# A block inverse by doubling: narrow column updates, a turned transpose, and scores issued first in each level

## The chip, the cores and the metric

The kernel runs on one core of a Trainium2 chip. The metric is device time of the whole program in microseconds (us); one launch computes everything.

## The reference, cut to what matters

The reference is two stacked networks over 256 tokens of width 1024. The change touches one mixer of the first, `even_mixer`, which runs once. Of it two parts matter: an attention of 8 heads of 64, and a gated delta rule of 4 heads of 128, whose core is a unit lower triangular solve.

```python
decay = jnp.exp(jnp.where(tri, gc[..., :, None] - gc[..., None, :], -jnp.inf))
a_mat = jnp.where(strict, jnp.einsum('bnhid,bnhjd->bnhij', k_beta, kc) * decay, 0.0)
t_mat = a_mat + jnp.eye(B_CHUNK, dtype=a_mat.dtype)
u = lax.linalg.triangular_solve(t_mat, vc * bc, left_side=True, lower=True, unit_diagonal=True)
w = lax.linalg.triangular_solve(t_mat, k_beta * jnp.exp(gc)[..., None], left_side=True, lower=True,
                                unit_diagonal=True)
```

The kernel takes chunks of 128 tokens instead of 64, which is the same function: two chunks T0 and T1, four heads each, so eight 128x128 matrices (I + A), and it needs the inverse X of each.

## The kernel before

Everything is float32. Each engine runs its own list of instructions in the order in which the code writes it, and semaphores join the lists; nothing is scheduled by a planner. In the mixer the functions are all called `even()`, one for each engine: ScalarE (L1034), VectorE (L1848), TensorE (L2729).

The inverse is built by doubling. For level 0 X = I - A masked to the pairs of rows. At level l (1 to 6) blocks of 2^l rows that are already inverted are joined in pairs: with `off` = A masked to the lower left quarters of the pairs (VectorE, `off(T, level)`, L1893), X becomes X - X (off X). The kernel keeps X in `d_X` and its transpose in `d_XT`, since a product on TensorE takes its left operand transposed as the weights. A level is, for each T:

- TensorE: Y = off X, four heads of 128 columns, into one PSUM bank (`LEV_Y`), L2875.
- ScalarE: copy of Y to SBUF (`quarter_copy`, L1087 to 1090), 128x512.
- TensorE: the product that changes XT (bank `LEV_XT`) and, up to level 5, the one that changes X (`LEV_X`), four heads each.
- VectorE: XT minus its bank (L1972), X minus its bank (L1974).

`each(bank, fn)` calls fn for the four heads, `product` (L2751) is one fp32 matmul of 128x128 by 128 columns and `turned` (L2754) one transpose against the identity. The trace shows an fp32 matmul as two passes, each a weight load and a matmul record, and a transpose as one.

Into these levels the attention heads are woven, one per level: `scores(i)` (TensorE, L2773 and 2774, weights of 64 rows), `masked(i)` (VectorE, L1867 to 1870: scale, mask and row maxima), `exps(i)` (ScalarE, L1078), `turn_p(i)` (TensorE, L2780, three transposes), `p_copy(i)` (ScalarE, L1085), `weigh(i)` (TensorE, L2788 to 2790, 64 columns), `head_out(i)` (VectorE, L1875 to 1877). TensorE's order in a level is Y of T0, Y of T1, `weigh(level)`, `scores(level + 1)`, XT and X of T0, the same of T1, `turn_p(level + 1)`.

The weights of the large projections come through a ring of seven 1 MB slots (`RING`), filled by the SP queue in order; a slot is loaded anew once ScalarE and VectorE have split both its halves, called granules, into a high part (`hi(k)`, L844) and a low part (`lo(k)`, L1595). On VectorE one `lo(2)` stands ahead of `masked(1)`, before the levels; it splits granules 2 and 3 of the mixer's output projection, which TensorE uses after the levels. Before the first level VectorE also copies X (L1963) from the PSUM banks 0 and 1, where TensorE has turned it from XT.

After the levels the products U and W are formed from XT (L2751 again, with `d_vb` and `d_kbg`), then the state, the normalisation and the output projection; then the feed-forward layer.

Of the kernel before, what the change touches and what calls it, by code (L numbers as in the profile page):

```python
# [24 lines left out]
ALU = mybir.AluOpType  # L25
ACT = mybir.ActivationFunctionType
# [143 lines left out]
def build_block_kernel(nc, t, const, out):  # L170

    ctx = ExitStack()
    with ctx:
# [271 lines left out]
        d_vn = [quarter(RAW, 0), buf(xt, 3)]  # L445
        d_S, d_U, d_W = quarter(RAW, 1), quarter(RAW, 5), buf(xt, 2)
        LEV_Y, LEV_XT, LEV_X = (4, 3), (2, 5), (0, 1)

        o_z = scr[:, 0:4096].rearrange("p (b n) -> p b n", b=TB)
        o_x = scr[:, 4096:8192].rearrange("p (b n) -> p b n", b=TB)  # L450
# [379 lines left out]
        def _(act):  # L830
# [203 lines left out]
            def even():  # L1034
# [39 lines left out]
                def exps(i):  # L1074

                    act.wait_ge(at_mx, n(at_mx))
                    for tb, k in ((0, slice(0, P)), (1, slice(P, 3 * P))):
                        ins = act.activation(a_s[:, i % 2, k], a_s[:, i % 2, k], ACT.Exp,  # L1078
                                             bias=w8(30 + i % 2, 2)[:, tb:tb + 1], accum_out=w8(32 + i % 2, 2)[:, tb:tb + 1])
                    ins.then_inc(at_p, 1)  # L1080

                def p_copy(i):

                    act.wait_ge(at_pt, n(at_pt))
                    act.activation(a_pt[:, i % 2, :], ps[:, 7, 0:384], ACT.Copy).then_inc(at_pc, 1)  # L1085

                def quarter_copy(dst, bank, wait, done):  # L1087

                    act.wait_ge(wait, n(wait))
                    act.activation(dst, ps[:, bank, :].rearrange("p (c n) -> p c n", c=4), ACT.Copy).then_inc(done, 1)  # L1090
# [74 lines left out]
                exps(0)  # L1165
                hi(2)
                p_copy(0)
                exps(1)
                p_copy(1)
                for level in range(1, 7):  # L1170
                    for T in range(TB):
                        quarter_copy(d_Y[T], LEV_Y[T], dl_y, dl_yc)
                    exps(level + 1)
                    p_copy(level + 1)
                n(dl_u)
# [382 lines left out]
        def _(dve):  # L1558
# [30 lines left out]
            def lo(k):  # L1589

                for g in range(gp[0] + ahead[0], gp[0] + k):
                    s = g // 2
                    c, width, o = granule(s, g % 2)
                    dve.wait_ge(hi_done, n.gran(g + 1))
                    dve.tensor_tensor(w_lo[:, g % SPLITS, 0:c * width], w_raw[:, s % RING, o:o + c * width],  # L1595
                                      w_hi[:, g % SPLITS, 0:c * width].bitcast(F32), ALU.subtract).then_inc(lo_done, 1)
                    if layer[0] is not None and at_sum[0] < (48 if layer[0] else 64):
                        credit[0] += SUM_RATE[layer[0]]
                        if credit[0] >= 1:
                            credit[0] -= 1  # L1600
                            accumulate(layer[0], at_sum[0])
                            at_sum[0] += 1
                gp[0] += k
                ahead[0] = 0
# [243 lines left out]
            def even():  # L1848
# [14 lines left out]
                def masked(i):  # L1863

                    dve.wait_ge(at_sc, n(at_sc))
                    m = w8(30 + i % 2, 2)
                    link(dve.scalar_tensor_tensor(a_s[:, i % 2, :], ps[:, 6, 0:384], A_DIM ** -0.5, e_mask, ALU.mult, ALU.add))  # L1867
                    dve.tensor_reduce(m[:, 0:1], a_s[:, i % 2, 0:P], AX_X, ALU.max)
                    link(dve.tensor_reduce(m[:, 1:2], a_s[:, i % 2, P:384], AX_X, ALU.max))
                    dve.tensor_scalar(m, m, -1.0, None, ALU.mult).then_inc(at_mx, 1)  # L1870

                def head_out(i):

                    dve.wait_ge(at_pv, n(at_pv))
                    link(dve.reciprocal(w8(34 + i % 2, 2), w8(32 + i % 2, 2)))  # L1875
                    for tb in range(TB):
                        ins = dve.tensor_scalar(xn[:, tb, i * A_DIM:(i + 1) * A_DIM], ps[:, 7, 384 + tb * A_DIM:384 + (tb + 1) * A_DIM],
                                                w8(34 + i % 2, 2)[:, tb:tb + 1], None, ALU.mult)
                    ins.then_inc(at_o, 1)
# [4 lines left out]
                def heads(b):  # L1884
                    return ps[:, b, :].rearrange("p (c n) -> p c n", c=4)
# [7 lines left out]
                def off(T, level):  # L1893

                    dve.tensor_tensor(d_off[T][level % 2], d_A[T], bc_mid(lev[:, level, :], 4), ALU.mult).then_inc(dl_off, 1)
# [60 lines left out]
                    dve.tensor_tensor(d_XT[T], bc_mid(ident, 4), d_Y[T], ALU.subtract).then_inc(dl_xt, 1)  # L1956
                    off(T, 1)
                head_out(0)
                lo(2)
                masked(1)  # L1960
                for T in range(TB):
                    dve.wait_ge(dl_xtt, n(dl_xtt))
                    dve.tensor_copy(d_X[T], heads((0, 1)[T])).then_inc(dl_x, 1)  # L1963
                for level in range(1, 7):
                    if level < 6:
                        off(0, level + 1)
                        off(1, level + 1)
                    head_out(level)
                    masked(level + 1)
                    for T in range(TB):  # L1970
                        dve.wait_ge(dl_xy, n(dl_xy))
                        ins = dve.tensor_tensor(d_XT[T], d_XT[T], heads(LEV_XT[T]), ALU.subtract)  # L1972
                        if level < 6:
                            ins = dve.tensor_tensor(d_X[T], d_X[T], heads(LEV_X[T]), ALU.subtract)  # L1974
                        ins.then_inc(dl_x, 1)
                dve.wait_ge(dl_u, 1)
                dve.tensor_copy(d_vn[0], heads(4)).then_inc(dl_vn, 1)
                head_out(7)
# [532 lines left out]
        def _(pe):  # L2511
# [217 lines left out]
            def even():  # L2729
# [14 lines left out]
                def each(bank, fn):  # L2744

                    for i in range(B_HEADS):
                        ins = fn(i, ps[:, bank, i * P:(i + 1) * P])
                    return ins

                def product(a, b):  # L2750
                    return lambda i, o: pe.matmul(o, a[:, i, :], b[:, i, :], start=True, stop=True)  # L2751
# [116 lines left out]
                pe.wait_ge(at_o, 1)  # L2868
                turn_p(1)

                for level in range(1, 7):
                    for T in range(TB):
                        pe.wait_ge(dl_off, n(dl_off))
                        pe.wait_ge(dl_x, n(dl_x))
                        each(LEV_Y[T], product(d_off[T][level % 2], d_X[T])).then_inc(dl_y, 1)  # L2875
                    weigh(level)
                    pe.wait_ge(at_mx, level + 1)
                    scores(level + 1)
                    for T in range(TB):
                        pe.wait_ge(dl_yc, n(dl_yc))  # L2880
                        ins = each(LEV_XT[T], product(d_Y[T], d_XT[T]))
                        if level < 6:
                            ins = each(LEV_X[T], product(d_XT[T], d_Y[T]))
                        ins.then_inc(dl_xy, 1)
                    pe.wait_ge(at_o, level + 1)
                    turn_p(level + 1)
# [557 lines left out]
```

## Time and profile before

| | |
|---|---|
| runs | 2714.8, 2716.03, 2716.27 us; median 2716.03 |
| profiled execution | 2714.96 us, span in the profile 2712.8 us |
| TensorE busy | 2622.0 us, 97% of the span, 12546 matmul records |
| VectorE, ScalarE busy | 2042.1 us (75%), 1681.3 us (62%) |
| DMA | 687.42 MB, mean 253 GB/s |
| the levels of the inverse | 328.15 to 375.71 us of the span |

The span begins with the first instruction and ends with the last one; the device time has 2.2 us around it. "PE" is TensorE's matmul, "PEld" its weight load, DVE is VectorE, ACT ScalarE. A number in brackets at the end of a timeline row is idle time of that engine before the row, with the instruction that ended it. The granted clock is the share of 2.4 GHz that TensorE got: 1.00, or 0.50 for 1.2 GHz. Matmuls overlap, so their lengths do not add up; the starts of the weight loads give TensorE's pace.

### The profile page before, as it was taken

To read this page: it belongs to the slowest core of one execution; us is meant where nothing else is said; L and a number is where in the kernel's file an instruction comes from. 1 tells how busy PE (TensorE), PEld (TensorE's weight loads), DVE (VectorE), ACT (ScalarE), POOL (GpSimd) and SP (SyncE) were. 2 spreads that over 40 slices of the span, in tenths; PEclk is the share of its full clock that TensorE was granted. 3 is DMA by queue.
4 is the path that set the end of the run, shared out by engine and by line. 5 is a ranking of instruction groups with operands and counts; after the bars stand their busy time and mean duration, and the time that the engine had idled before them with its cause. 6 is when DMAs were issued, how large, how long until landed. Compare 5 with 4: busy or idle time off the path is not lost.

```text
span 2712.8 us, 35093 instructions
## 1 busy us (share of the span) xinstructions
PE 2622.0 (97%) x12546; PEld 2159.3 (80%) x12546; DVE 2042.1 (75%) x2376; ACT 1681.3 (62%) x2188; POOL 155.0 (6%) x196
## 2 busy tenths in 40 slices
PE   7999899999999999999989999999999999999997
PEld 6888787888887887888767888788887878888886
DVE  4556657777766765554577875799999999999998
ACT  4446645454456765454464444678788787878786
POOL 2000000000000000003310000300000000000020
PEclk9999999999999999999999999899999999999999
DMA  8554306768744346754128884699999999999995
GB/s 291 190 171 163 109 32 241 248 223 299 261 162 158 125 130 238 269 172 138 63 84 307 314 289 148 225 378 372 367 387 362 388 357 378 372 378 373 361 390 223
DMA packets 284412, 687.42 MB, mean 253 GB/s; under 512 B 13428, under 2 KB 21904, under 8 KB 284304
## 3 DMA queue, kind: packets, MB, share of 16 engines
q1 hardware_dynamic: 266032, 618.65, 63.7%
q0 software_dynamic: 18272, 67.32, 7.0%
q8 instruction: 69, 1.13, 0.2%
q14 instruction: 39, 0.32, 0.0%
HBM read 670.19 MB, written 15.73 MB: 253 GB/s over the span
## 4 chain that ended last, share of the span: by engine, by line
PE 84%; DVE 8%; ACT 5%; issue 2%; DMA 0%; DVEq 0%; SPq 0%; ACTq 0%; POOL 0%
PE ps L2519 26%; PE ps L2521 25%; PE ps L2520 25%; DVE w_lo L1595 2%; PE ps L2667 2%; ACT w_hi L844 2%; PE ps L2751 1%; DVE xt L2365 1%; DVE xn L1674 1%; DVE h L1679 1%; PE ps L3137 0%; DVE act_lo L1663 0%; ACT hp L1257 0%; PE ps L3203 0%; PE ps L2726 0%
## 5 line engine op out<-in xcount | busy, mean ns | idle before, releaser
L1595 DVE TENSOR_TENSOR w_lo<-w_raw,w_hi 128x1024 fp32r<-128x1024 f32 x1158 | 1397.4, 1226 | 424.3 <-ACT w_hi L844 394.1
L844 ACT ACTIVATE w_hi<-w_raw 128x1024 fp32r<-128x1024 f32 x1158 | 1211.7, 1057 | 773.4 <-PE ps L2521 772.8
L2519 PE MATMUL ps<-w_hi,act_hi 128*128 128x512 f32 (+1 forms) x3424 | 1343.9, 392 | 39.0 <-DVE w_lo L1595 23.3
L2521 PE MATMUL ps<-w_lo,act_hi 128*128 128x512 f32 (+1 forms) x3424 | 1321.8, 386 | 0.0
L2520 PE MATMUL ps<-w_hi,act_lo 128*128 128x512 f32 (+1 forms) x3424 | 1320.4, 386 | 0.0
L2519 PEld LDWEIGHTS ps<-w_hi,act_hi 128*128 128x128 f32 x3424 | 646.8, 189 | 183.6 <-DVE w_lo L1595 36.8
L2521 PEld LDWEIGHTS ps<-w_lo,act_hi 128*128 128x128 f32 x3424 | 646.4, 189 | 131.5
L2520 PEld LDWEIGHTS ps<-w_hi,act_lo 128*128 128x128 f32 x3424 | 647.2, 189 | 123.4 <-issue 1.4
L1586 DVE SCALAR_TENSOR_TENSOR scr<-scr,small 128x1024 f32<-128x1024 f32 x98 | 125.2, 1278 | 0.0
L1002 ACT ACTIVATE act_hi<-ps 128x512 fp32r<-128x512 f32 (+1 forms) x87 | 62.5, 719 | 64.2 <-PE ps L2667 64.2
L1720 DVE TENSOR_TENSOR act_lo<-ps,act_hi 128x512 fp32r<-128x512 f32 (+1 forms) x87 | 74.0, 850 | 34.7 <-ACT act_hi L1002 34.7
L647 POOL DMA_DIRECT2D scr<-in_ada_w x48 | 33.9, 706 | 844.7 <-DVE scr L1586 458.6
L2667 PEld LDWEIGHTS ps<-cst,hp 128*128 128x128 f32 x456 | 54.0, 140 | 21.1 <-DVE hp L1743 6.9
L2667 PE MATMUL ps<-cst,hp 128*128 128x128 f32 x456 | 64.5, 273 | 6.0 <-DVE hp L1743 5.4
L1743 DVE SCALAR_TENSOR_TENSOR hp<-ps,rn,sg 128x512 f32<-128x512 f32 (+1 forms) x48 | 31.7, 701 | 36.7 <-PE ps L2521 36.7
L1747 DVE TENSOR_TENSOR hp<-sg,ps 128x512 f32<-128x512 f32 (+1 forms) x63 | 46.6, 739 | 8.1 <-PE ps L2521 8.1
L780 POOL TENSOR_TENSOR dtw<-dtw 128x4 f32<-128x4 f32 x1 | 0.8, 827 | 853.7 <-DMA rows_out<-scr 853.7
L1024 ACT ACTIVATE sg<-ps 128x512 f32<-128x512 f32 (+1 forms) x63 | 39.6, 629 | 0.1
L1020 ACT ACTIVATE sg<-ps,rn 128x512 f32<-128x512 f32 (+1 forms) x48 | 28.3, 639 | 11.4 <-PE ps L2521 11.4
L887 ACT ACTIVATE act_hi<-ps,colv 128x128 fp32r<-128x128 f32 x96 | 26.5, 375 | 9.4 <-PE ps L2549 9.4
L1663 DVE SCALAR_TENSOR_TENSOR act_lo<-ps,colv,act_hi 128x128 fp32r<-128x128 f32 x96 | 26.3, 341 | 3.2 <-ACT act_hi L887 3.2
L2230 DVE TENSOR_REDUCE small<-ps 128x2 f32<-128x1024 f32 x16 | 19.4, 1220 | 7.2 <-PE ps L3203 6.9
(513 smaller groups left out, 1419.5 us busy)
## 6 DMA issues: line engine op xcount, KB each, us to landing
w_raw<-in_moe_w SPq DMA_DIRECT2D x337, 1024.0 KB, 6.8
scr<-in_ada_w POOLq DMA_DIRECT2D x48, 1024.0 KB, 6.7
w_raw<-in_ffn_w_gate SPq DMA_DIRECT2D x44, 1024.0 KB, 5.3
w_raw<-in_ffn_w_up SPq DMA_DIRECT2D x44, 1024.0 KB, 5.6
w_raw<-in_ffn_w_down SPq DMA_DIRECT2D x44, 1024.0 KB, 5.0
w_raw<-in_ff_w SPq DMA_DIRECT2D x42, 1024.0 KB, 5.5
w_raw<-in_odd_w_in SPq DMA_DIRECT2D x20, 1024.0 KB, 5.2
w_raw<-in_even_w_in SPq DMA_DIRECT2D x14, 1024.0 KB, 5.2
```

The lines of the kernel that those rows point to most:

```text
L647: pool.dma_start(m_w[:, j % 2], src).then_inc(ada_in[j % 2], 16)
L844: act.activation(w_hi[:, g % SPLITS, 0:c * width], w_raw[:, s % RING, o:o + c * width], ACT.Copy).then_inc(hi_done, 1)
L1002: act.activation(act_hi[:, base:base + c, 0:tbs * P], src, ACT.Copy).then_inc(hhi_done, 1)
L1024: act.activation(sg[:, 0:tbs * BANK].rearrange("p (b n) -> p b n", b=tbs)[:, :, 0:width], ps[:, 4:4 + tbs, 0:width], ACT.Silu).then_inc(si ...
L1586: dve.scalar_tensor_tensor(dst, w, x, dst, ALU.mult, ALU.add).then_inc(ada_sum, 1)
L1595: dve.tensor_tensor(w_lo[:, g % SPLITS, 0:c * width], w_raw[:, s % RING, o:o + c * width], w_hi[:, g % SPLITS, 0:c * width].bitcast(F32), ...
L1720: dve.tensor_tensor(act_lo[:, base:base + c, 0:tbs * P], src, act_hi[:, base:base + c, 0:tbs * P].bitcast(F32), ALU.subtract).then_inc(hlo ...
L1747: dve.tensor_tensor(view[0], view[1], ps[:, 6:6 + tbs, 0:width], ALU.mult).then_inc(hid_done, 1)
L2519: pe.matmul(out_ap, hi, whi, start=start, stop=False)
L2520: pe.matmul(out_ap, lo, whi, start=False, stop=False)
L2521: return pe.matmul(out_ap, hi, wlo, start=False, stop=stop)
L2667: ins = pe.transpose(banks(6, tbs)[:, o:o + P], hp[:, tb * BANK + k * P:tb * BANK + k * P + P], ident)
```

## The change

X is updated only in the columns that a level changes. Of each pair of blocks these are the columns of the first block, `first_columns(x, level)`: runs of 2^level columns out of every 2^(level+1), 64 of a head's 128 at every level. Y = off X is formed for them alone, into half a bank, packed; ScalarE copies the 64 columns per head (`d_Yc`); the X product is formed from them, and VectorE subtracts 128x256 numbers in place of 128x512. The XT product goes. Instead TensorE turns X (`turned(d_X[T])`) from level 2 on, right behind Y of the same T, and ScalarE copies the turned matrix to `d_XT`. At level 6 only the lower left 64x64 of X is missing, and it is subtracted straight from XT, rows 0 to 63 and columns 64 to 127.

The first copies of X go from VectorE to ScalarE. TensorE issues `scores(level + 1)` first in a level, and VectorE runs `masked(level + 1)` ahead of `off` and `head_out(level)`. The `lo(2)` ahead of `masked(1)` goes to level 6, in the place of `off`.

```diff
--- before.py
+++ after.py
@@ -445,6 +445,20 @@
         d_vn = [quarter(RAW, 0), buf(xt, 3)]
         d_S, d_U, d_W = quarter(RAW, 1), quarter(RAW, 5), buf(xt, 2)
         LEV_Y, LEV_XT, LEV_X = (4, 3), (2, 5), (0, 1)
+        LEVELS = 6
+        d_Yc = [y[:, :, 0:64] for y in d_Y]
+
+        def first_columns(x, level):
+
+            return x.rearrange("p c (b two s) -> p c b two s", two=2, s=1 << level)[:, :, :, 0, :]
+
+        def packed(x, level):
+
+            return x.rearrange("p c (b s) -> p c b s", s=1 << level)
+
+        def half_bank(b):
+
+            return ps[:, b, 0:256].rearrange("p (c n) -> p c n", c=4)
         o_z = scr[:, 0:4096].rearrange("p (b n) -> p b n", b=TB)
         o_x = scr[:, 4096:8192].rearrange("p (b n) -> p b n", b=TB)
@@ -1165,11 +1179,16 @@
                 exps(0)
                 hi(2)
                 p_copy(0)
+                for T in range(TB):
+                    quarter_copy(d_X[T], T, dl_xtt, dl_x)
                 exps(1)
                 p_copy(1)
-                for level in range(1, 7):
+                for level in range(1, LEVELS + 1):
                     for T in range(TB):
-                        quarter_copy(d_Y[T], LEV_Y[T], dl_y, dl_yc)
+                        act.wait_ge(dl_y, n(dl_y))
+                        act.activation(d_Yc[T], half_bank(LEV_Y[T]), ACT.Copy).then_inc(dl_yc, 1)
+                        if level > 1:
+                            quarter_copy(d_XT[T], LEV_XT[T], dl_xtt, dl_yc)
                     exps(level + 1)
                     p_copy(level + 1)
                 n(dl_u)
@@ -1956,23 +1975,22 @@
                     dve.tensor_tensor(d_XT[T], bc_mid(ident, 4), d_Y[T], ALU.subtract).then_inc(dl_xt, 1)
                     off(T, 1)
                 head_out(0)
-                lo(2)
                 masked(1)
-                for T in range(TB):
-                    dve.wait_ge(dl_xtt, n(dl_xtt))
-                    dve.tensor_copy(d_X[T], heads((0, 1)[T])).then_inc(dl_x, 1)
-                for level in range(1, 7):
-                    if level < 6:
+                for level in range(1, LEVELS + 1):
+                    masked(level + 1)
+                    if level < LEVELS:
                         off(0, level + 1)
                         off(1, level + 1)
+                    else:
+                        lo(2)
                     head_out(level)
-                    masked(level + 1)
                     for T in range(TB):
                         dve.wait_ge(dl_xy, n(dl_xy))
-                        ins = dve.tensor_tensor(d_XT[T], d_XT[T], heads(LEV_XT[T]), ALU.subtract)
-                        if level < 6:
-                            ins = dve.tensor_tensor(d_X[T], d_X[T], heads(LEV_X[T]), ALU.subtract)
-                        ins.then_inc(dl_x, 1)
+                        if level < LEVELS:
+                            x, y = first_columns(d_X[T], level), packed(half_bank(LEV_X[T]), level)
+                        else:
+                            x, y = d_XT[T][0:64, :, 64:128], half_bank(LEV_X[T])[0:64]
+                        dve.tensor_tensor(x, x, y, ALU.subtract).then_inc(dl_x, 1)
                 dve.wait_ge(dl_u, 1)
                 dve.tensor_copy(d_vn[0], heads(4)).then_inc(dl_vn, 1)
                 head_out(7)
@@ -2868,19 +2886,32 @@
                 pe.wait_ge(at_o, 1)
                 turn_p(1)
-                for level in range(1, 7):
-                    for T in range(TB):
-                        pe.wait_ge(dl_off, n(dl_off))
-                        pe.wait_ge(dl_x, n(dl_x))
-                        each(LEV_Y[T], product(d_off[T][level % 2], d_X[T])).then_inc(dl_y, 1)
-                    weigh(level)
+                def narrow(bank, level, fn):
+
+                    for i in range(B_HEADS):
+                        ins = fn(i, packed(half_bank(bank), level)[:, i])
+                    return ins
+
+                for level in range(1, LEVELS + 1):
                     pe.wait_ge(at_mx, level + 1)
                     scores(level + 1)
                     for T in range(TB):
-                        pe.wait_ge(dl_yc, n(dl_yc))
-                        ins = each(LEV_XT[T], product(d_Y[T], d_XT[T]))
-                        if level < 6:
-                            ins = each(LEV_X[T], product(d_XT[T], d_Y[T]))
+                        off, x, xt_, y = d_off[T][level % 2], first_columns(d_X[T], level), d_XT[T], d_Yc[T]
+                        pe.wait_ge(dl_off, n(dl_off))
+                        pe.wait_ge(dl_x, n(dl_x))
+                        narrow(LEV_Y[T], level, lambda i, o: pe.matmul(o, off[:, i, :], x[:, i], start=True, stop=True)).then_inc(dl_y, 1)
+                        if level > 1:
+                            each(LEV_XT[T], turned(d_X[T])).then_inc(dl_xtt, 1)
+                    weigh(level)
+                    for T in range(TB):
+                        off, x, xt_, y = d_off[T][level % 2], first_columns(d_X[T], level), d_XT[T], d_Yc[T]
+                        pe.wait_ge(dl_yc, n(dl_yc, 2 if level > 1 else 1))
+                        if level < LEVELS:
+                            ins = narrow(LEV_X[T], level,
+                                         lambda i, o: pe.matmul(o, xt_[:, i, :], packed(y, level)[:, i], start=True, stop=True))
+                        else:
+                            ins = narrow(LEV_X[T], level,
+                                         lambda i, o: pe.matmul(o[0:64, 0], y[:, i, :], xt_[:, i, 64:128], start=True, stop=True))
                         ins.then_inc(dl_xy, 1)
                     pe.wait_ge(at_o, level + 1)
                     turn_p(level + 1)
```

## Rows read from the trace of the kernel before

**Rows 1.** The page, the chain that ended last: shares of the span by engine.
```profile
PE 84%; DVE 8%; ACT 5%; issue 2%; DMA 0%; DVEq 0%; SPq 0%; ACTq 0%; POOL 0%
```

**Rows 2.** Busy time by stretch: columns as printed; then granted clock, DMA share, GB/s.
```profile
core 0: us, PE busy (x) PEld busy (x) DVE busy (x) ACT busy (x) POOL busy (x), PEclk, DMA share, GB/s
309.40:311.90 2.50, 2.50 (x23) 2.50 (x24) 0.18 (x1) 2.50 (x7) 0.00 (x0) 1.00 0.01 3
321.60:331.80 10.20, 4.74 (x21) 4.37 (x22) 7.70 (x15) 2.07 (x6) 0.00 (x0) 0.50 0.33 104
345.01:352.85 7.84, 7.59 (x64) 7.03 (x63) 5.76 (x13) 2.67 (x7) 0.00 (x0) 1.00 0.01 3
250.30:253.30 3.00, 3.00 (x29) 3.00 (x29) 2.81 (x4) 3.00 (x7) 0.00 (x0) 1.00 0.01 3
```

**Rows 3.** Timeline of one level, weight loads: start, length, line, count, idle before.
```profile
352.85 0.36 PEld L2780 LDWEIGHTS ps<-cst,scr 128*128 128x128 f32 x3
353.18 0.97 PEld L2751 LDWEIGHTS ps<-scr 128*128 128x128 f32 x8
...
354.56 0.97 PEld L2751 LDWEIGHTS ps<-xt 128*128 128x128 f32 x8 [0.41 <-issue]
355.45 0.30 PEld L2788 LDWEIGHTS ps<-scr 128*128 128x128 f32 x2
355.67 0.30 PEld L2789 LDWEIGHTS ps<-scr 128*128 128x128 f32 x2
...
356.26 0.29 PEld L2773 LDWEIGHTS ps<-scr 64*128 64x128 f32 x2
...
357.11 1.86 PEld L2751 LDWEIGHTS ps<-scr 128*128 128x128 f32 x16 [0.33 <-issue]
```

**Rows 4.** Timeline of the front, to the load of `turn_p(2)`.
```profile
323.35 2.35 DVE L1595 TENSOR_TENSOR w_lo<-w_raw,w_hi 128x1024 fp32r<-128x1024 f32 x2
...
325.61 0.55 DVE L1867 SCALAR_TENSOR_TENSOR scr<-ps,scr 128x384 f32<-128x384 f32 x1
...
327.05 0.40 ACT L1078 ACTIVATE scr<-scr,small 128x128 f32<-128x128 f32 x1 [7.72 <-DVE small L1870]
...
328.15 0.50 PEld L2780 LDWEIGHTS ps<-cst,scr 128*128 128x128 f32 x3 [5.14 <-issue]
...
328.63 1.83 PEld L2751 LDWEIGHTS ps<-scr 128*128 128x128 f32 x8
...
337.18 0.36 PEld L2780 LDWEIGHTS ps<-cst,scr 128*128 128x128 f32 x3
```

**Rows 5.** Whole run, groups by shape: busy us, mean ns, idle before.
```profile
L1221 ACT ACTIVATE xt<-ps,colv 128x256 f32<-128x256 f32 x16 | 7.7, 562 | 3.2 <-PE ps L2937 3.2
...
L1244 ACT ACTIVATE xt<-ps 128x256 f32<-128x256 f32 x4 | 1.5, 364 | 0.0
...
L2081 DVE SCALAR_TENSOR_TENSOR act_lo<-ps,colv,act_hi 128x256 fp32r<-128x256 f32 x12 | 5.0, 476 | 0.0
```

**Rows 6.** Timeline of the level of rows 3, ScalarE and VectorE.
```profile
354.38 0.60 ACT L1090 ACTIVATE scr<-ps 128x512 f32<-128x512 f32 x1 [0.40 <-PE ps L2751]
...
357.22 0.56 DVE L1867 SCALAR_TENSOR_TENSOR scr<-ps,scr 128x384 f32<-128x384 f32 x1 [0.17 <-PE ps L2774]
...
358.46 0.17 DVE L1870 TENSOR_SCALAR small<-small 128x2 f32<-128x2 f32 x1
```

**Rows 7.** Timeline of weight loads, an 8-column projection, at half clock.
```profile
253.66 0.33 PEld L2519 LDWEIGHTS ps<-w_hi,act_hi 128*128 128x128 f32 x1
253.88 0.33 PEld L2520 LDWEIGHTS ps<-w_hi,act_lo 128*128 128x128 f32 x1
```

**Rows 8.** Timeline of weight loads, `turn_p(6)` and the first product after the loop.
```profile
368.51 0.36 PEld L2780 LDWEIGHTS ps<-cst,scr 128*128 128x128 f32 x3
...
375.71 0.97 PEld L2751 LDWEIGHTS ps<-sg,scr 128*128 128x128 f32 x8
```

**Rows 9.** The page, DMA issues: count, size of one, median us to landing.
```profile
w_raw<-in_ffn_w_gate SPq DMA_DIRECT2D x44, 1024.0 KB, 5.3
```

## The prediction

> **What bounds the kernel now.** I read the page first, then the timeline of the stretch in which the changed lines run (about 323 to 376 us), then its clock, then what each engine waits for there. The page's chain [rows 1] gives TensorE 84% of the time, so the kernel is one long stream of TensorE work; the inverse is only some 50 us of 2713, and what the change is worth is decided there alone. One level of the loop repeats every 7.84 us at full clock with TensorE busy 7.59 of it [rows 2]. The reader can lay the level out by the starts of the weight loads [rows 3]: three transposes `turn_p` at 352.85; Y of T0 at 353.18 (eight loads in 0.97, so 0.111 a pass, 0.89 for four fp32 products of two passes each); a stall of 0.49 until VectorE has written X of T1; Y of T1 at 354.56, 0.89; `weigh` at 355.45, products of 64 columns; `scores` at 356.26; the XT and X products from 357.11, 32 passes in 3.57. Sum: 0.33 + 0.89 + 0.49 + 0.89 + 0.81 + 0.85 + 3.57 = 7.83. So a level is bound by TensorE's passes, with one short wait.
>
> The first level is another matter [rows 4]. VectorE splits two weight granules (`lo(2)`, 323.35, 2.35 us) ahead of `masked(1)` (325.61). ScalarE's exponentials wait for that (327.05), and TensorE's `turn_p(1)` waits for them (328.15, after 5.14 us without a load). In this idle time the granted clock is at half, 1.2 GHz, and stays there to 331.8 (0.50 over 321.6 to 331.8 [rows 2]), 3.65 us after TensorE resumed.
>
> **Part 1: what a narrow product costs.** The change makes Y and X 64 columns wide. The price of a pass is what matters, and the nearest row is `weigh`, which also moves 64 columns through 128x128 weights: L2788 begins at 355.45, L2789 at 355.67, so 0.22 for two passes, the same 0.111 as 128 columns [rows 3]. With 8 columns TensorE still makes 29 loads in 3.00 us, about 0.107 apart (250.3 to 253.3 [rows 2]). So halving the columns saves nothing by itself: a narrow product stays at 0.22. Bounds: not below that; above it, if reading every other run of X (`first_columns`, runs of 2 to 64 elements) is slow, up to a doubled 0.44. No row has such a stepped operand; I take 0.22, the row it is nearest to.
>
> **Part 2: what goes and comes on TensorE per level (2 to 5).** Removed: eight wide XT products, 8 x 0.22 = 1.78. Added: eight transposes, 8 x 0.11 = 0.89 (three of them take 0.33 at 352.85 [rows 3]). So the passes fall by 0.89. `scores` moves to the front of the level and the turns lie between the two Y, which together cover what was the stall for X of T1 (0.49 gone). The 64-row weights of `scores` load only as the last matmul before them ends: 0.15 later than the spacing alone behind `weigh` (355.45 + 3 x 0.22 = 356.11 against 356.26 [rows 3]); behind the three transposes I count 0.19. New level: `turn_p` 0.33, drain 0.19, `scores` 0.85, Y 0.89, transposes 0.44, Y 0.89, transposes 0.44, `weigh` 0.67, X 0.89 + 0.89 = **6.48 us**, 1.35 less than 7.83.
>
> Is anything else late in 6.48? Count from `turn_p`'s first load. ScalarE: Y of T0 is finished near 2.5 and copied as 128x256 (0.36 to 0.56 by forms of that size [rows 5]; a 512-element copy takes 0.60 [rows 6], so I take 0.39) to about 2.95; XT of T0 to 3.6; Y and XT of T1 to 4.3 and 4.9. X of T0 starts at 4.70 and of T1 at 5.59, so both are covered, T1 by 0.7. Behind these four copies stand the exponentials, 1.1 us with their read-outs to the load they release (327.05 to 328.15 [rows 4]): to 6.0, and the next `turn_p` is due at 6.48, 0.5 of room. VectorE: `masked` from 1.5, 1.4 long (357.22 to 358.46 and 0.17 [rows 6]), two masks `off` 1.3, `head_out` after `weigh` to about 5.7, then the two X updates of 128x256 at 0.42 (0.48 by the nearest form [rows 5]) to 6.2 and 7.2; the next Y of T0 wants the first at 7.85. So it stays with TensorE. If the ScalarE copies take 0.56 instead of 0.39 the room falls to 0.1 and costs nothing. Four levels: 4 x 1.35 = **5.4 us**.
>
> **Part 3: the front.** `lo(2)` leaves its place, so `masked(1)` starts 2.26 us earlier (325.61 - 323.35 [rows 4]), and with it the exponentials and `turn_p(1)`: load at 325.89 for 328.15. The X copies that go from VectorE to ScalarE (two of 0.60) run at 319.8 and 323.5, where ScalarE is idle before the exponentials. **2.26 us** gained.
>
> **Part 4: level 1 and the clock.** Before, from `turn_p(1)` to `turn_p(2)` it took 9.03 (328.15 to 337.18 [rows 4]), nearly four microseconds of it at half clock: the sixteen Y passes took about 0.21 each (the first eight loads in 1.83). Narrow passes double at half clock too: of the 8-column passes two loads lie 0.22 apart at 253.66 and 253.88 [rows 7], half as far until 253.3 [rows 2]. When does the clock rise now? If at the same instant as before (331.8): `turn_p` 0.48 and its drain 0.35, `scores` 1.5, both Y 3.45, then at full clock `weigh` 0.7 and X 1.78: 8.3 us, `turn_p(2)` at 334.2. If as long after the resumption as before (3.65 us, at 329.5): about 1.0 less. There is no XT turn in level 1. I take the late end, **0.75 us** gained, as the low stretch began before the part that changes; the early end would give 1.75.
>
> **Part 5: level 6 and `lo(2)`'s new place.** Before: 7.2 us from `turn_p(6)` at 368.51 to the first product after the loop at 375.71 [rows 8]. Now `turn_p`, drain, `scores`, Y, turns and `weigh` reach 4.70; the X products with 64 columns of weights have no row: between 0.45 and 0.89 for each T. VectorE: `masked(7)` to 2.95, `lo(2)` 2.35 to 5.3, `head_out(6)` 0.7 to 6.0, the update of T0 to 6.4. So here VectorE ends last, and the product after the loop starts at 6.45 whichever X costs. **0.75 us** gained. The moved `lo(2)` frees a slot of the weight ring some 38 us later, and SP's load behind it starts that much later; it is a slot of the second gate step of the feed-forward, needed after 400, and one such load lands in 5.3 us [rows 9], so it is hidden. TensorE wants these two granules only after the loop.
>
> **The sum.** 2.26 + 0.75 + 5.4 + 0.75 = 9.2 us. The profiled execution took 2714.96, which gives 2705.8; the median of the runs shown is 2716.03, 1.1 higher, which gives 2706.8. I forecast **2706.3**. What follows the loop (the state chain, then the feed-forward, TensorE-bound) shifts as a whole.
>
> **Rival 1, slower: the clock falls inside the loop.** Each new level consists of 64-column passes and transposes. At 253.3 the clock fell with TensorE never idle, after a run of nothing but 8-column passes [rows 2, 7]: a busy engine with thin work can lose it. If it fell for the whole loop, a level would cost double its passes: about 12.2 us, 4.4 more than 7.83. Four such levels, +17.5, level 6 +4, less 3.0 at the front: +18.5, **2734**. It decides from about two levels: each low level turns 1.35 gained into 4.4 lost. Against it: 24 transposes and nothing else between 309.4 and 311.9 ran at a granted 1.00 [rows 2], and the new level has no idle time, with wide `scores` in it. 7%.
> The Trainium skill ("TensorE: Matmul & The Clock Gate", Part 4: PE-mode transpose) says that transposes do not count as work for the clock gate as matmuls do. By that rule the eight new transposes would thin the level further and the time would be this rival's 2734; the stretch from 309.4 does not bear it out.
>
> **Rival 2, no change: stepped reads are slow.** If every Y pass on every other run takes twice its slot, Y costs 1.78 more per level: 5 x 1.78 = 8.9 less gain in levels 2 to 6 and some 1 in level 1: **2716**, same as before. For it: no row shows such an operand. Against: a 64-column pass needs half the time that its slot has (128 columns fit in it), so a doubled read would still fit. If it bites only where runs are 2 or 4 long, 2 to 3 us go. 7% in full.
>
> **Rival 3: the loop becomes a chain of hand-overs.** The four copies, exponentials and `turn_p` have 0.5 of room. If copies and hand-overs together cost 1.2 more than I count, the level is 7.2 and the gain 2.26 + 4 x 0.63 + 1.0 = 5.8: **2710**. For it: five hand-overs in a row in each level. Against: the copies are shorter than before. 14%.
>
> **Chances.** Forecast 72%, rival 1 7%, rival 2 7%, rival 3 14%. This kernel's runs tell a change from none at about 0.2%, 5.4 us. The forecast and three quarters of rival 3 lie beyond it: 0.82 faster; rival 2 and the rest of rival 3, 0.11 same; rival 1, 0.07 slower. Range: if the shorter idle time left the clock at full for all of level 1 (5.7 in place of 8.3, 2.6 more gained), the time were 2703.2 from the profiled execution, and the low end is a little below; rival 3 reaches to 2711.5, part of rival 2 with it.
>
> **What the changed profile would show.** The first load of `turn_p` repeats every 6.5 us in levels 2 to 5 (right) or 7.2 and more (rival 3, with ScalarE's exponentials as the releaser). Eight loads of a narrow Y in 0.97 (part 1), or 1.9 at a clock of 1.00 (rival 2). The first load of `turn_p(1)` near 325.9. A granted clock of 1.00 from 331.8 on to the end of the loop; 0.50 there is rival 1. No idle time before Y of T1. In level 6, VectorE's update as the releaser of the first product behind the loop, near 366.5. The prediction is wrong if a narrow pass is not 0.111, if the clock falls between 332 and 367, or if TensorE stands later for the moved weight load.

## The result, and the profile after

The changed kernel takes 2726.26 us in the median of 20 runs (2718.36 to 2737.47), the kernel before 2714.37 (2711.38 to 2719.47): a ratio of 1.0047, 95% interval 1.0033 to 1.0060, so 12 us slower. The forecast was 2706.3. The 20 runs fall in two groups, eleven of 2718.4 to 2726.3 and nine of 2733.4 to 2737.5; the profiled execution, 2734.03 us, is of the slower group, and e5 below has one of the faster.

The page of the changed kernel, its span, busy times, the granted clock in 40 slices and the chain's shares:

```profile
span 2732.2 us, 35013 instructions
...
PE 2646.1 (97%) x12506; PEld 2179.4 (80%) x12506; DVE 2032.8 (74%) x2364; ACT 1685.7 (62%) x2200; POOL 152.7 (6%) x196
...
PEclk9999869999999999999999999999999999999999
...
PE 85%; DVE 8%; ACT 5%; issue 2%; DMA 0%; DVEq 0%; SPq 0%; ACTq 0%; POOL 0%
```

Fewer matmul records than before (12506 for 12546) and yet 24 us more of busy TensorE. The sixth digit of the clock row is a 6; that slice is 342 to 410 us, and the loop lies in and ahead of it.

Busy time by stretch in the changed kernel (columns as in [rows 2]); level 1 with the 1.2 us ahead of it, level 2, level 6, and the whole low stretch:

```profile
324.10:335.70 11.60, 10.33 (x45) 9.38 (x45) 3.71 (x11) 3.11 (x11) 0.00 (x0) 0.50 0.01 1
335.70:347.71 12.01, 12.01 (x55) 11.03 (x56) 4.02 (x11) 3.33 (x9) 0.00 (x0) 0.50 0.00 0
...
383.73:394.57 10.84, 10.84 (x55) 9.62 (x56) 5.07 (x11) 3.32 (x9) 0.00 (x0) 0.50 0.30 96
324.10:395.80 71.70, 70.43 (x316) 64.33 (x317) 25.26 (x67) 20.03 (x57) 0.00 (x0) 0.50 0.05 15
```

TensorE is never idle in levels 2 to 6, but at a clock of 0.50. Levels 2 to 5 take 12.0 us each, where the kernel before needed 7.84 [rows 2]. The low clock lasts from 324.1 to 395.8, 71.7 us; before it lasted 10.2. It ends 0.75 us after the first product behind the loop (395.05).

Level 3 of the changed kernel, weight loads, to be read beside [rows 3]:

```profile
347.71 0.66 PEld L2798 LDWEIGHTS ps<-cst,scr 128*128 128x128 f32 x3
348.69 0.50 PEld L2791 LDWEIGHTS ps<-scr 64*128 64x128 f32 x2 [0.33 <-issue]
...
350.27 1.78 PEld L2902 LDWEIGHTS ps<-scr 128*128 128x128 f32 x8 [0.65 <-issue]
351.82 0.87 PEld L2772 LDWEIGHTS ps<-cst,scr 128*128 128x128 f32 x4
352.67 1.83 PEld L2902 LDWEIGHTS ps<-xt,scr 128*128 128x128 f32 x8
354.27 0.87 PEld L2772 LDWEIGHTS ps<-cst,xt 128*128 128x128 f32 x4
...
356.41 1.83 PEld L2911 LDWEIGHTS ps<-scr 128*128 128x128 f32 x8
358.12 1.83 PEld L2911 LDWEIGHTS ps<-scr,xt 128*128 128x128 f32 x8
359.71 0.44 PEld L2798 LDWEIGHTS ps<-cst,scr 128*128 128x128 f32 x2
```

Eight loads of a narrow product span 1.83 us, 0.21 apart, twice the 0.97 of [rows 3]: the same passes, each half as fast. The order is the new one (`turn_p`, `scores`, Y, turn, Y, turn, `weigh`, X, X).

The front, to be read beside [rows 4] (ScalarE's second copy of X, VectorE's start of `masked(1)`, the exponentials, the loads of `turn_p(1)` and of `turn_p(2)`):

```profile
322.45 0.60 ACT L1104 ACTIVATE xt<-ps 128x512 f32<-128x512 f32 x1 [2.66 <-PE ps L2772]
322.81 0.55 DVE L1886 SCALAR_TENSOR_TENSOR scr<-ps,scr 128x384 f32<-128x384 f32 x1
...
324.24 0.40 ACT L1092 ACTIVATE scr<-scr,small 128x128 f32<-128x128 f32 x1 [1.19 <-DVE small L1889]
...
325.34 0.50 PEld L2798 LDWEIGHTS ps<-cst,scr 128*128 128x128 f32 x3 [3.16 <-issue]
...
335.70 0.66 PEld L2798 LDWEIGHTS ps<-cst,scr 128*128 128x128 f32 x3
```

The longest sum of waits within the loop (engine, line, for whom; total, times, longest), ScalarE's copy of Y:

```profile
ACT scr L1189 <- PE ps L2902: 24.2, 12, 3.0
```

It waits for TensorE, as VectorE does, while TensorE has from 328 on only short gaps between weight loads, 0.7 us at most, and none of them ends on another engine: no hand-over is late.

### The profile page after: what moved, and what is told of

Its sections match the earlier page's. It is cut to its first block, busy times and chain, and to the rows that moved or that the text cites. A ratio compares the mean times of both kernels' runs of the same rounds, so it can differ in the third digit from the quotient of the medians.

```text
span 2732.2 us, 35013 instructions
## 1 busy us (share of the span) xinstructions
PE 2646.1 (97%) x12506; PEld 2179.4 (80%) x12506; DVE 2032.8 (74%) x2364; ACT 1685.7 (62%) x2200; POOL 152.7 (6%) x196
## 4 chain that ended last, share of the span: by engine, by line
PE 85%; DVE 8%; ACT 5%; issue 2%; DMA 0%; DVEq 0%; SPq 0%; ACTq 0%; POOL 0%
PE ps L2537 26%; PE ps L2539 25%; PE ps L2538 25%; DVE w_lo L1614 2%; PE ps L2685 2%; ACT w_hi L858 2%; PE ps L2902 1%; DVE xt L2383 1%; PE ps L2911 1%; DVE xn L1693 1%; DVE h L1698 1%; PE ps L3168 0%; DVE act_lo L1682 0%; ACT hp L1276 0%; PE ps L3234 0%
## 5 line engine op out<-in xcount | busy, mean ns | idle before, releaser
L1034 ACT ACTIVATE sg<-ps,rn 128x512 f32<-128x512 f32 (+1 forms) x48 | 28.3, 639 | 11.3 <-PE ps L2539 11.3
```

## Experiments

All times are medians; each ratio is to runs of the kernel before on the same chip. Each experiment has one profiled execution, so a stretch shown is that execution's; where the runs of a kernel lie close together, it can stand for them. Two theories stood at first. **A**: the clock is lost in the idle time ahead of level 1, as it was before, and passes of 64 columns do not bring it back; where it is at full, they keep it. **B**: the passes of 64 columns lose it by themselves. **C**, the rival to both: the clock is not the point, but the order, the turned transpose or the moved split.

**e1: the same passes, 128 columns wide.**

```diff
-narrow(LEV_Y[T], level, lambda i, o: pe.matmul(o, off[:, i, :], x[:, i], start=True, stop=True)).then_inc(dl_y, 1)
+each(LEV_Y[T], product(off, d_X[T])).then_inc(dl_y, 1)
...
 if level < LEVELS:
-    ins = narrow(LEV_X[T], level,
-                 lambda i, o: pe.matmul(o, xt_[:, i, :], packed(y, level)[:, i], start=True, stop=True))
+    ins = each(LEV_X[T], product(xt_, d_Y[T]))
 else:
-    ins = narrow(LEV_X[T], level,
-                 lambda i, o: pe.matmul(o[0:64, 0], y[:, i, :], xt_[:, i, 64:128], start=True, stop=True))
+    ins = each(LEV_X[T], product(d_Y[T], xt_))
```

These are TensorE's lines. ScalarE's copy of Y is 128x512 again, and VectorE subtracts the same 64 columns, read out of a full bank.

> The changed kernel with its Y and X products over all 128 columns of a head again (same number of products and passes); the numbers outside the changed columns are computed and not used. The copy of Y is 128x512 again, VectorE subtracts the 64 columns only. Theory A (the clock is lost in the idle time ahead of level 1 and passes of 64 columns cannot raise it again) and theory B (passes of 64 columns lose it by themselves): the clock is back at 1.00 some 7 us after the loop begins, at full clock a level takes 6.5 us, the kernel 2705 to 2707. Theory C (the lost time is the order of the loop, the turned transpose or the moved split, not the width): still slower than the kernel before, 2720 or more.

Measured: 2706.0 us against 2713.76, ratio 0.9974 (0.9962 to 0.9985). Busy time by stretch, the low stretch at the front, then two levels:

```profile
319.80:326.60 6.80, 4.65 (x17) 3.70 (x18) 3.01 (x10) 1.63 (x6) 0.00 (x0) 0.50 0.01 2
329.67:336.15 6.48, 6.48 (x55) 5.98 (x54) 4.02 (x11) 3.53 (x9) 0.00 (x0) 1.00 0.00 0
336.15:342.64 6.49, 6.49 (x55) 5.99 (x54) 4.02 (x11) 3.52 (x9) 0.00 (x0) 1.00 0.00 0
```

The clock is down for 6.8 us, 319.8 to 326.6, and a level takes 6.48. Theory C is out: order, turns and moved split are all in this kernel, and it is 20 us faster than the changed one. What differs is the width, in the direction of more arithmetic (with it ScalarE's copy, for which TensorE does not wait in the levels of either kernel). All seven runs lie at 2704.6 to 2707.8, all 20 of the changed kernel at 2718.4 or more.

**e2: wide fillers ahead of level 1, the narrow loop kept.**

```diff
+for _ in range(8):
+    pe.matmul(ps[:, 5, :], ones, d_A[0].rearrange("p c n -> p (c n)"), start=True, stop=True)
 for level in range(1, LEVELS + 1):
```

> The changed kernel with eight useless fp32 matmuls of 512 columns ahead of level 1, in a free PSUM bank; they cost 6.8 us at half clock, 3.4 at full. Theory A: they raise the clock, the narrow levels then hold it at 1.00, 6.5 us each, and the kernel takes about 2709, faster than before although it does more. Theory B: the clock is raised and falls again within one or two levels, levels of 12 us, 2735 or more.

Measured: 2713.4 us against 2713.76, ratio 0.9998 (0.9989 to 1.0007). Busy time by stretch, the low stretch, level 2, level 6:

```profile
321.10:331.30 10.20, 6.86 (x13) 3.44 (x14) 3.16 (x10) 2.07 (x6) 0.00 (x0) 0.50 0.01 2
340.78:347.13 6.35, 6.35 (x56) 5.85 (x56) 4.02 (x11) 3.32 (x9) 0.00 (x0) 1.00 0.00 0
...
366.18:372.02 5.84, 5.84 (x56) 5.20 (x56) 4.66 (x11) 3.32 (x9) 0.00 (x0) 1.00 0.01 3
```

The fillers cost more than I had counted: 9.5 us (326.23 to 335.75, level 1 with them 15.3) for a counted 6.8 at most. Eight fp32 matmuls are 16 passes, and a pass of 512 columns takes 0.43 us at full clock (e6's loads at 315.85 and 316.28); the expectations here and of e6 took 0.43 for a whole matmul. So the time is 4 us over the expected 2709. What decides between A and B is the clock: it rises under the fillers, at 331.3, and stays at 1.00 through the narrow levels, 6.35 us each, and 5.84 up to `turn_p(7)` in the last. B is out.

**e3: transposes as fillers, and e9: narrow products as fillers**, in the same place, 32 passes each.

```diff
+for _ in range(8):
+    each(5, turned(d_A[0]))
```

```diff
+for _ in range(4):
+    each(5, lambda i, o: pe.matmul(o[:, 0:64], d_A[0][:, i, :], d_A[0][:, i, 0:64], start=True, stop=True))
```

> The same with 32 useless transposes of 128x128 in place of the eight matmuls, as long at half clock (32 x 0.213 = 6.8 us). If transposes count for the clock as products do: the same picture as with the matmuls, the clock at 1.00 before or early in level 1 (about 2709 under theory A). If they do not: the clock stays at 0.50 through the loop, and the kernel takes the changed kernel's time and 6.8 us more, 2730 to 2744.

> The same place as the useless matmuls and the useless transposes, with 16 useless fp32 products of 64 columns, 32 passes, 6.8 us at half clock like those. Theory A, with the width as the reason why the clock does not return: these passes do not raise it either; the clock stays at 0.50 over the filler and into the loop, and the kernel takes the changed kernel's time and up to 6.8 us more, 2724 to 2744. If any busy TensorE raises it after enough time: as the transposes did, 2706 to 2714.

Measured: e3 2708.61 us against 2713.76, ratio 0.9983 (0.9974 to 0.9992); e9 2742.2 against 2714.34, ratio 1.0101 (1.0086 to 1.0117). The fillers in e3's timeline and their stretch, with what follows:

```profile
322.40 5.78 PE L2772 MATMUL ps<-cst,scr 128*128 128x128 f32 x32
```

```profile
322.50:326.60 4.10, 4.10 (x21) 4.10 (x20) 0.00 (x0) 0.49 (x1) 0.00 (x0) 0.50 0.02 4
326.80:333.10 6.30, 6.30 (x54) 5.80 (x53) 3.59 (x10) 1.64 (x6) 0.00 (x0) 1.00 0.00 0
```

The same in e9:

```profile
326.17 6.93 PE L2896 MATMUL ps<-scr 128*128 128x64 f32 x32
```

```profile
326.00:333.00 7.00, 7.00 (x34) 6.91 (x32) 0.00 (x0) 0.49 (x1) 0.00 (x0) 0.50 0.01 2
333.00:345.00 12.00, 12.00 (x50) 10.46 (x49) 4.02 (x11) 2.13 (x7) 0.00 (x0) 0.50 0.00 0
324.40:402.70 78.30, 77.20 (x348) 71.32 (x349) 25.15 (x66) 20.05 (x57) 0.00 (x0) 0.50 0.04 14
```

Each has 32 passes in one unbroken run, 5.8 us of 128-column transposes and 6.9 us of 64-column products, TensorE without a gap in both. Under the transposes the clock rises, at 326.7; under the narrow products it stays at 0.50, and beyond them to the end of the loop. The time differs by 34 us, and no run of one comes near the other (e3 2705.6 to 2714.1, e9 2741.6 to 2744.9). The pair differs in the kind of pass as well as in its width; that the width by itself is enough is e1's and e8's to show, where the same products are only made wider.

**e5: the changed kernel once more**, for another execution in the profile.

> The changed kernel itself, for a second profile and its spread (2718 to 2737 so far). Theory A: the clock is at 0.50 for a part of the loop that differs by execution; where the profile is of a shorter execution, the clock comes back inside the loop and the levels after it take 6.4 us. If the spread lies elsewhere, the loop looks the same in every profile (levels of 12 us) and the difference is outside 318 to 400 us.

Measured: 2719.42 us against 2713.4, ratio 1.0049 (1.0024 to 1.0073), five runs at 2718.8 to 2719.4 or 2734.6 to 2734.7; the profiled one took 2718.83. Busy time by stretch, level 1 with the front, level 2, and levels 4 and 5:

```profile
318.80:333.41 14.61, 11.44 (x48) 10.09 (x49) 6.62 (x19) 3.71 (x12) 0.00 (x0) 0.50 0.01 1
333.41:345.42 12.01, 12.01 (x55) 11.03 (x55) 4.01 (x11) 3.32 (x9) 0.00 (x0) 0.50 0.00 0
...
355.31:361.65 6.34, 6.34 (x56) 5.84 (x55) 4.02 (x11) 3.32 (x9) 0.00 (x0) 1.00 0.00 1
361.65:368.00 6.35, 6.35 (x56) 5.85 (x55) 4.02 (x11) 3.32 (x9) 0.00 (x0) 1.00 0.00 0
```

Level 4's loads in the same execution:

```profile
355.31 0.37 PEld L2798 LDWEIGHTS ps<-cst,scr 128*128 128x128 f32 x3
355.84 0.29 PEld L2791 LDWEIGHTS ps<-scr 64*128 64x128 f32 x2 [0.17 <-issue]
...
356.69 0.97 PEld L2902 LDWEIGHTS ps<-scr 128*128 128x128 f32 x8 [0.33 <-issue]
...
361.65 0.37 PEld L2798 LDWEIGHTS ps<-cst,scr 128*128 128x128 f32 x3
```

Here the clock came back at 352.9, in the middle of level 3, and the narrow levels after it kept it and took 6.35 us. So theory A holds only in a weaker form: the narrow levels keep the clock from returning for 34 us here and for the whole loop in the other profile, but not for good.

The spread of the changed kernel is in the main the instant of that return. From `turn_p(0)` to the first product behind the loop this execution took 59.29 us (314.83 to 374.12), the slower one 77.93: 18.6 apart, for spans 15.3 apart. The mean granted clock of the 20 runs says the same, 0.983 to 0.985 at 2718 to 2719 us and 0.977 at 2736 to 2737. Against the 58.06 of the kernel before, this loop lost only 1.2 us of a span 4.1 longer; the rest lies outside, where this profile has longer half-clock stretches near 830 and 865 us (10 and 7 us) than that of the kernel before (3.4 each). What decides in the loop when the clock returns, I did not settle.

**e8: only the X products wide**, in levels 1 to 5. Y stays at 64 columns. TensorE's line (VectorE reads the bank accordingly):

```diff
-    ins = narrow(LEV_X[T], level,
-                 lambda i, o: pe.matmul(o, xt_[:, i, :], packed(y, level)[:, i], start=True, stop=True))
+    ins = each(LEV_X[T], lambda i, o: pe.matmul(o, xt_[:, i, :], d_Y[T][:, i, :], start=True, stop=True))
```

> The changed kernel with only the X products of levels 1 to 5 over 128 columns; the Y products stay at 64. As many passes, so the same 6.4 to 6.5 us a level at full clock. Theory A with the width as the cause: half the wide products are between the changed kernel and the first experiment; either they raise the clock in the first levels (2706 to 2710) or they do it only in some executions, with the median between 2710 and 2726.

Measured: 2709.89 us against 2713.4, ratio 0.9980 (0.9971 to 0.9989), eleven runs of 2704.9 to 2711.2. Busy time by stretch, the low stretch and level 2:

```profile
321.00:334.70 13.70, 10.29 (x43) 8.94 (x44) 6.40 (x19) 3.71 (x12) 0.00 (x0) 0.50 0.01 1
335.37:341.76 6.39, 6.39 (x56) 5.89 (x55) 4.02 (x11) 3.32 (x9) 0.00 (x0) 1.00 0.00 0
```

Half of the products wide is enough to bring the clock back, 13.7 us after its fall instead of 6.8 in e1. It lies between the two, as expected.

**e6: the idle time ahead of level 1 filled, the narrow loop kept; e7: the same with the wide products.** Two, two and four useless matmuls stand where TensorE waits.

```diff
 turn_p(0)
-pe.wait_ge(dl_xt, 1)
 pe.wait_ge(dl_tc, 7)
+wide(0, 2)
+pe.wait_ge(dl_xt, 1)
...
 scores(1)
+wide(4, 2)
 pe.wait_ge(dl_xt, 2)
 pe.wait_ge(dl_dt, 2)
 each(1, turned(d_XT[1])).then_inc(dl_xtt, 1)
+wide(5, 4)
```

`wide(bank, count)` is count times an fp32 matmul of 512 columns into that bank.

> The changed kernel with useless fp32 matmuls of 512 columns in TensorE's idle times ahead of level 1 only: two, two and four of them, 0.43 us each at full clock, where it waits 0.8, 1.1 and 2.0 us. Theory A: the clock does not fall ahead of the loop, all six narrow levels run at 1.00, level 1 takes 5.7 us, and the kernel 2703 to 2705, the fastest so far. Theory B: it falls inside the loop, 2720 or more.

> The same fillers with the products of 128 columns of the first experiment. Theory A and B: clock at 1.00 from the front through the loop, levels of 6.5 us, 2703 to 2705; against the first experiment's 2706 some 2 us less, all of it in level 1. If the fillers cost more than they save, 2706 or more.

Measured: e6 2702.86 us against 2713.4, ratio 0.9963 (0.9949 to 0.9976), the fastest of all; e7 2703.47, ratio 0.9961 (0.9948 to 0.9975). e6's stretches, front, level 1, level 2:

```profile
315.09:324.40 9.31, 9.31 (x39) 5.22 (x38) 6.77 (x15) 3.69 (x9) 0.00 (x0) 1.00 0.15 59
324.40:330.28 5.88, 5.88 (x47) 5.09 (x46) 3.59 (x10) 2.13 (x7) 0.00 (x0) 1.00 0.01 3
330.28:336.63 6.35, 6.35 (x56) 5.85 (x55) 4.02 (x11) 3.32 (x9) 0.00 (x0) 1.00 0.00 0
```

The clock does not fall ahead of the loop and not in it. Level 1 takes 5.88 us. The change, with eight matmuls that compute nothing, is 10.5 us faster than the kernel before.

**e4: the moved split alone**, in the kernel before, and **e10: the fillers alone**, in the kernel before.

```diff
 head_out(0)
-lo(2)
 masked(1)
...
         off(1, level + 1)
+    else:
+        lo(2)
     head_out(level)
```

> The kernel before with one edit of the change: lo(2) goes from ahead of masked(1) to level 6 of the loop. All theories: turn_p(1) 2.3 us earlier, clock back at full in level 1 since the products are wide; 2712 to 2713 against 2714 to 2715, 2.3 us less. If the move itself costs the change its time (the weight load behind it comes late), this kernel is slower than the one before.

> The kernel before with the useless matmuls in TensorE's idle times ahead of level 1 (two, two, four), nothing else. It prices the front's half clock alone: level 1 of the kernel before had four us of its 9 at half clock, so 1.5 to 2.5 us less, 2711 to 2712 against 2713 to 2714. If the gain of the change with these fillers (10.5 us) came from the fillers and not from the narrow loop, this kernel would show it, 2704 or less.

Measured: e4 2715.36 us against 2713.76, ratio 1.0006 (0.9997 to 1.0015), with one run of 5301.79 that stands alone; e10 2714.19 against 2714.34, ratio 1.0001 (0.9992 to 1.0010). e4's low stretch at the front, its level 2, and a later low stretch:

```profile
319.10:325.90 6.80, 3.97 (x18) 3.60 (x19) 5.06 (x13) 1.71 (x6) 0.00 (x0) 0.50 0.01 2
331.67:339.50 7.83, 7.58 (x63) 7.02 (x62) 5.75 (x13) 2.67 (x7) 0.00 (x0) 1.00 0.00 0
411.20:414.50 3.30, 3.30 (x9) 2.58 (x8) 2.68 (x10) 3.24 (x7) 0.00 (x0) 0.51 0.92 321
```

Its level 2 takes 7.83 as before, and from `turn_p(0)` to `turn_p(7)` it takes 55.13 us in the profile (314.79 to 369.92) where the kernel before took 57.78 (317.65 to 375.43). e10 took 56.04 (317.50 to 373.54). So the profiled executions show 2.7 and 1.7 us saved in the loop, and the medians show neither; the expectations of e4 (2.3 us less) and of e10 (1.5 to 2.5 less) are both missed, though e10's clock is at 1.00 through front and loop. e10 says that the fillers by themselves give nothing measurable: the 10.5 us of e6 are the new loop's own, once it has its clock, and e7 shows that the narrow products are no part of them that could be measured. Where the small savings of e4 went is open; its profile has a half-clock stretch from 411.2 where the kernel before has none between 405 and 420. Such a short stretch between 401 and 429 us is also in the profiles of e1, e2, e3, e5 and e7, and in none of the changed kernel, e6, e8, e9 and e10; all of these but e10 have the moved split, so it does not bring the stretch by itself. Outside the front and the loop the profiled executions spend between about 46 us (the kernel before, e6, e10) and 60 (e2) at half clock, about 50 in e4, and that alone can hide a saving of two or three.

## Why the prediction was wrong

**The step that failed is part 4**, "I take the late end": that the clock comes back at 331.8 as before, with level 1 gaining 0.75 us and the rest of the loop at full clock; and with it rival 1's wording, "the clock falls inside the loop". Both asked only when the clock would rise and whether it would fall inside the loop. It was down before the loop began, which part 4 had seen. Ahead of the rise at 331.8 the kernel before ran 3.2 us of 128-column Y passes [rows 4]; the change makes just these narrow, and the same loop with wide products has its clock back at 326.6 (e1). The changed kernel goes from 324.1 on at 0.50 to behind the loop, in the profile of e5 from 318.8 to 352.9. Rival 1's price for the whole loop at half clock was right, 2734 with levels of 12.2 us: the profiled execution took 2734.03 with levels of 12.0, nine of 20 runs 2733.4 or more, the median 2726.26. Its cause was not: nothing falls in the loop. The narrow passes keep a full clock through the loop (e2, e6) and a low one for 34 to 78 us (e5, the changed kernel, e9). I gave it 7% because I judged it by stretches that ran at full clock, and those say nothing of how one gets back.

**Part 1 was right, and wrong in its use.** A narrow pass costs what a wide one does at full clock, 0.89 for eight, and stepped reads of X cost nothing (rival 2 is out). But from "halving the columns saves nothing by itself" follows that on TensorE the narrowing could only lose something, and I did not look for what.

**Part 2 was right to 0.01 us** for wide products: 6.48 forecast, 6.48 in e1. With narrow ones, for which it was forecast, the level is 6.35, 0.13 less; no run here says why. Rival 3, the chain of hand-overs, did not appear; ScalarE's copy of 128x256 took 0.39.

**Part 3 was right.** From `turn_p(0)` to `turn_p(1)`: 10.50 us before (317.65 to 328.15), 8.22 after (317.12 to 325.34), 2.28 less; forecast 2.26.

**Part 4's size.** From `turn_p(1)` to `turn_p(2)`: 9.03 before, 8.3 forecast, 10.36 measured (325.34 to 335.70), all of it at half clock. So level 1 lost 1.3 us for a forecast gain of 0.75, and levels 2 to 5 lost 4.2 each for a forecast gain of 1.35. With the clock at full level 1 is 5.88 (e6), 5.7 by the end of the range.

**Part 5.** Before, 7.2 us from `turn_p(6)` to the first product behind the loop; forecast 6.45; in e6 6.12 (355.67 to 361.79), in the changed kernel 11.3 at half clock (383.73 to 395.05). The end of level 6 in the changed kernel, `lo(2)`, SP's load, X of T0, the first instruction of `head_out(6)`, VectorE's update of T0:

```profile
387.72 2.35 DVE L1614 TENSOR_TENSOR w_lo<-w_raw,w_hi 128x1024 fp32r<-128x1024 f32 x2
...
390.14 0.37 SPq L612 DMA_DIRECT2D w_raw<-in_ffn_w_gate  x1
...
392.67 1.12 PE L2914 MATMUL ps<-scr 128*64 128x64 f32 x8
392.78 0.17 DVE L1894 RECIPROCAL small<-small 128x2 f32<-128x2 f32 x1 [2.71 <-PE ps L2808]
...
393.82 0.41 DVE L1993 TENSOR_TENSOR scr<-scr,ps 64x256 f32<-64x256 f32 x1 [0.37 <-PE ps L2914]
```

`head_out(6)` waited for `weigh`, not for `lo(2)`, since at half clock TensorE was the later one. At full clock VectorE is last, as forecast: in e6 its update of T0 starts at 361.34, takes 0.40, and the product behind the loop loads at 361.79. The load of SP is issued at 390.14 for 325.77 before, 64 us later (35 in e6, where 38 was counted), and no engine waits for it. The 64-column weights had no row before; at half clock eight such passes take 0.90 (392.67 to 393.58) against 1.71 for full weights.

**The sum over the loop.** From `turn_p(0)` to the first product behind the loop: 58.06 before (317.65 to 375.71), 77.93 after (317.12 to 395.05), 46.81 in e6 (314.98 to 361.79). The 19.9 us between the first two stand beside 19.1 between the profiled executions. The 11.2 of e6 stand against 11.8, the forecast's 9.2 and 2.6 more for a full level 1 as the range had it: the front gave 1.1 for 2.3, as the fillers take time in it, level 1 3.2 for 3.4, levels 2 to 5 5.9 for 5.4, level 6 1.1 for 0.75. The errors partly cancel.

The forecast of 2706.3 is near what e1 measures, 2706.0, and e1's loop saves 9.3 us in the profile (58.06 less 48.75) for a forecast 9.2 (2.3 in the front, 1.3 in level 1, 5.4 in levels 2 to 5, 0.4 in level 6). So the mechanism of the gain stood, in the kernel with the wide products. That the two times meet is luck in part: the forecast started from 2714.96 and 2716.03, while the kernel before has a median of 2713.76 beside e1, so e1's gain is 7.8 us in medians.

The Trainium skill ("TensorE: Matmul & The Clock Gate", Part 4: PE-mode transpose) has it that transposes do not count for the clock gate as matmuls do. The trace disagrees: 32 transposes brought the clock from 0.50 to 1.00 (e3), where 32 products of 64 columns did not (e9).

## What to carry to other kernels

Where the weight load sets the pace of a pass, fewer columns save no time and can cost the clock: keep the products wide and narrow only what is read out. Judge a change by the clock that TensorE has when it arrives there, and ask what brings it back up if it is down; a loop that keeps a full clock may be unable to regain one. A few useless wide matmuls in the waits ahead of such a loop can be worth more than the narrowing.

## What the runs showed of the hardware that I had not expected

- Weight loads slow with the clock: loads of 128 columns start 0.107 to 0.111 us apart at 1.00 and 0.21 at 0.50, also where the product moves 64 columns only (the changed kernel). A pass of 512 fp32 columns takes 0.43 us at 1.00 (e6), so 64 columns are moved in about 0.054, an estimate from that row: half of the time of a narrow pass. The Trainium skill ("TensorE: Matmul & The Clock Gate", LDWEIGHTS (loading the stationary operand)) prices a load by its columns over 1.2, 107 ns here, and names no clock; the starts of the loads agree with it at 1.00 and lie twice as far apart at 0.50.
- TensorE stayed at 0.50 for 71.7 us (the changed kernel) and 78.3 (e9), busy all the time but for 1.3 and 1.1 us; in another execution of the changed kernel the clock came back after 34.1 us (e5).
- The same loop runs its levels at 1.00 in 6.35 us if it has the full clock at its start (e6), and in 12.0 if it has not, for all six levels or for the first ones.
- Reading every other run of columns cost nothing, down to runs of two numbers. Y of T0 in level 1 of e6, its weight loads, eight in 0.97 us:

```profile
326.09 0.97 PEld L2911 LDWEIGHTS ps<-scr 128*128 128x128 f32 x8 [0.33 <-issue]
```
